# Up projections of a decoder kernel: one product of 512 columns with the high weights, four banks, and stages entered by halves

## The chip, the cores and the metric

The kernel runs on one core of one Trainium2 chip. Its time is the device time of one execution in microseconds (us). Three runs of the kernel before took 1253.54 to 1254.74 us, with a median of 1254.59 us.

## The reference

The reference is a decoder of four layers on one sequence of 256 tokens with 1024 features, all float32. Each layer adds a mixer and then an MLP to x. Layers 0 and 3 have a gated linear recurrence (eight heads), layer 1 block attention, layer 2 a pooling over windows of 2, 4, 8 and 16 tokens.

```python
def rmsnorm(x, gain):
    xf = x.astype(jnp.float32)
    y = xf * lax.rsqrt(jnp.mean(xf * xf, axis=-1, keepdims=True) + RMS_EPS)
    return (y * gain.astype(jnp.float32)).astype(x.dtype)

def sqrelu_mlp(h, w1, w2):          # w1: 1024 x 4096, w2: 4096 x 1024
    a = jax.nn.relu(h @ w1)
    return (a * a) @ w2

for i in range(DEPTH):
    h = rmsnorm(x, norm_mix[i])
    ...                             # y = the mixer of the layer
    x = x + y.astype(x.dtype)
    x = x + sqrelu_mlp(rmsnorm(x, norm_mlp[i]), mlp_w1[i], mlp_w2[i]).astype(x.dtype)
return rmsnorm(x, norm_final)
```

## The kernel before

x is kept transposed, features on the partitions: `xT` has 8 k tiles of 128 features by 256 tokens. A float32 operand goes to TensorE as two numbers of type float32r, a high and a low part. For weights ScalarE writes the high part (`whi`, L929) and VectorE the low part (`wlo = raw - whi`, L1260). For x it is `xh` (L942, with the gain of the norm as its scale) and `xl` (L1271). A product of two such operands is three products: high by high, high by low, low by high. The factor rstd of the norm does not depend on the feature, so it is applied behind the projection; it comes from the sum of squares (`ones_mm`, L453), is made by ScalarE (`rms`), and is turned into a column per token by two transposes (`token_column`, L462, copied into `rcol` by VectorE, L1289).

All weights pass through one ring of two slots, in groups of 2 MB. A group has two units of 1 MB, each loaded by one transfer and split by one ScalarE and one VectorE operation of 128 x 2048. `split(g)` does both units, `split_unit(g, u)` one. Each engine has its own program in the order written here, and waits on semaphores: `lo_done` counts low parts, `bank_ready` finished banks of PSUM, `x_ready` updates of x (four for each addition, of two k tiles each), `xl_done` the low parts of x.

PSUM has eight banks of 512 columns: `hb` (2), `acc` (4) and `misc` (2). `out_banks` are both `hb` and both `misc`.

The MLP of a layer works on 8 pieces of 512 hidden features. The up projection of a piece (`mlp_up`, one group of weights) makes four tiles of 128 features by 256 tokens; `hb[0]` holds tiles 0 and 1, `hb[1]` tiles 2 and 3. For each tile and k tile it issues three products of 256 columns (L559, L560, L561), 96 in all. `hidden` makes the activation for each bank: ScalarE relu (L1217), VectorE multiply by rstd (L1674) and square (L1679), ScalarE high part `hh` (L1223), VectorE low part `hl` (L1681). The down projection of a piece (`mlp_down`, L589 to L591, also 96 products) adds into the four `acc` banks. TensorE's order is up 0, up 1, down 0, then a loop up k+1, down k, and the last down. ScalarE and VectorE have the splits of the coming groups in their order around each `hidden`.

A stage begins with `take_x`: VectorE updates x by two k tiles at a time (L1656 after a mixer, L1717 after an MLP, L1650 after the pooling), ScalarE makes `xh`, VectorE `xl`, and a dictionary says after which step the splits of the next group stand. `group(..., early=...)` issues a mixer's group of weights in two banks; in layer 1 and in the first up projection of each layer the first bank begins with k tiles 0 to 5. `norm_steps` puts `ones_mm` and `token_column` between the quarters of a mixer's first group. In layers 0 and 3 the gates that follow (`gate_a` to `gate_c`) need `rcol`; they run on ScalarE and VectorE in turn, and TensorE's `e_step` (L660) needs their results (`lf_ready`) and those of L1383.

## Time and profile before

| What | Value |
|---|---|
| median of 3 runs | 1254.59 us |
| the profiled execution | 1255.52 us, its span 1253.4 us |
| granted TensorE clock, mean | 0.988 |
| TensorE busy | 1206.9 us (96%), 9363 products |
| VectorE busy | 803.2 us (64%) |
| ScalarE busy | 630.3 us (50%) |
| GpSimd busy | 42.7 us (3%) |
| moved between memory and core | 202.55 MB, mean 162 GB/s |
| `xh` of one k tile (L942), 64 times | mean 499 ns alone, 0.45 us in a pair |
| high part of a unit (L929), 186 times | mean 1903 ns |
| low part of a unit (L1260), 186 times | mean 2317 ns |

The profiled execution is one run with the hardware profiler; its time is a little above its span, which goes from the first to the last instruction. Busy times of TensorE overlap from one product to the next, since a product is still in the array when the next one starts. So the cost of a product in a row of products is the distance of their starts, or a stretch divided by its number of products, and not its mean duration. "Granted clock" is the share of 2.4 GHz that the chip gave to TensorE.

### The profile page before, as it was taken

What the parts mean: (1) busy time and instruction counts of PE and PEld (TensorE: products, weight loads), DVE (VectorE), ACT (ScalarE), POOL (GpSimd) and SP (SyncE); (2) the same over time, 40 slices, a digit from 0 to 9 for tenths busy, and PEclk for the clock granted to TensorE, in tenths of its full rate; (3) what the DMA queues carried; (4) which work ended last, traced back from release to release, by engine and by line L of the source; (5) the groups of instructions that cost most, each with busy time, mean ns of one, the idle gap of its engine ahead of it and who ended that gap; (6) DMA issues with size and microseconds to landing.
All of it is one profiled execution on the core that took longest, in us unless ns stands there. A gap on an engine that the chain in (4) does not pass through costs nothing.

```text
span 1253.4 us, 22191 instructions
## 1 busy us (share of the span) xinstructions
PE 1206.9 (96%) x9363; PEld 1170.1 (93%) x9363; DVE 803.2 (64%) x808; ACT 630.3 (50%) x707; POOL 42.7 (3%) x40
## 2 busy tenths in 40 slices
PE   6999899999999999999997999999989989999997
PEld 5999889999999999999996999999878989999997
DVE  6777767655666656656557675556877767655654
ACT  6955564444453445444435444445885575534441
POOL 2000010000010001000001100000100001000000
PEclk9999999999999999999998899999999999999999
DMA  9442344645356444545445355545433324554520
GB/s 340 153 135 101 101 135 142 225 171 191 144 204 217 142 130 152 202 171 195 171 152 200 124 191 199 192 174 193 160 109 106 121 78 147 191 201 161 200 108 34
DMA packets 84594, 202.55 MB, mean 162 GB/s; under 512 B 3253, under 2 KB 5383, under 8 KB 84272
## 3 DMA queue, kind: packets, MB, share of 16 engines
q1 hardware_dynamic: 84496, 201.58, 46.4%
q8 instruction: 50, 0.82, 0.3%
q14 instruction: 16, 0.13, 0.0%
q0 software_dynamic: 32, 0.02, 0.0%
HBM read 200.52 MB, written 1.06 MB: 161 GB/s over the span
## 4 chain that ended last, share of the span: by engine, by line
PE 84%; DVE 8%; ACT 4%; issue 2%; DMA 1%; SPq 0%; DVEq 0%; ACTq 0%
PE hb L559 10%; PE hb L561 10%; PE hb L560 10%; PE acc L589 9%; PE acc L591 9%; PE acc L590 9%; PE hb L511 4%; PE hb L514 4%; PE hb L513 4%; DVE wlo L1260 3%; PE acc L672 2%; PE hb L527 2%; PE hb L528 2%; PE hb L526 2%; ACT whi L929 1%
## 5 line engine op out<-in xcount | busy, mean ns | idle before, releaser
L1260 DVE TENSOR_TENSOR wlo<-raw,whi 128x2048 fp32r<-128x2048 f32 x186 | 425.1, 2317 | 197.6 <-ACT whi L929 197.5
L929 ACT ACTIVATE whi<-raw 128x2048 fp32r<-128x2048 f32 x186 | 347.0, 1903 | 144.1 <-PE acc L591 121.2
L559 PE MATMUL hb<-xh,whi 128*128 128x256 f32 x1024 | 293.0, 286 | 7.0 <-DVE xT L1656 2.9
L561 PE MATMUL hb<-xh,wlo 128*128 128x256 f32 x1024 | 291.1, 284 | 0.0
L560 PE MATMUL hb<-xl,whi 128*128 128x256 f32 x1024 | 291.1, 284 | 0.0
L589 PE MATMUL acc<-arena_r,whi 128*128 128x256 f32 x1024 | 290.4, 284 | 0.0
L591 PE MATMUL acc<-arena_r,wlo 128*128 128x256 f32 x1024 | 290.0, 283 | 0.0
L590 PE MATMUL acc<-arena_r,whi 128*128 128x256 f32 x1024 | 289.9, 283 | 0.0
L559 PEld LDWEIGHTS hb<-xh,whi 128*128 128x128 f32 x1024 | 197.8, 193 | 8.5 <-DVE xT L1656 3.3
L560 PEld LDWEIGHTS hb<-xl,whi 128*128 128x128 f32 x1024 | 197.8, 193 | 0.1
L561 PEld LDWEIGHTS hb<-xh,wlo 128*128 128x128 f32 x1024 | 197.8, 193 | 0.0
L589 PEld LDWEIGHTS acc<-arena_r,whi 128*128 128x128 f32 x1024 | 196.7, 192 | 0.6 <-DVE wlo L1260 0.6
L591 PEld LDWEIGHTS acc<-arena_r,wlo 128*128 128x128 f32 x1024 | 196.7, 192 | 0.0
L590 PEld LDWEIGHTS acc<-arena_r,whi 128*128 128x128 f32 x1024 | 196.7, 192 | 0.0
L511 PE MATMUL hb<-xh,whi 128*128 128x256 f32 x384 | 111.5, 290 | 0.6 <-DVE wlo L1260 0.5
L514 PE MATMUL hb<-xh,wlo 128*128 128x256 f32 x384 | 108.7, 283 | 0.0
L513 PE MATMUL hb<-xl,whi 128*128 128x256 f32 x384 | 108.6, 283 | 0.0
L1674 DVE TENSOR_TENSOR arena<-arena,rstd 128x512 f32<-128x512 f32 x64 | 44.2, 691 | 89.0 <-ACT arena L1217 71.7
L1217 ACT ACTIVATE arena<-hb 128x512 f32<-128x512 f32 x64 | 38.0, 594 | 121.9 <-PE hb L561 121.9
L1223 ACT ACTIVATE arena_r<-arena 128x512 fp32r<-128x512 f32 x64 | 40.5, 632 | 109.3 <-DVE arena L1679 109.3
L511 PEld LDWEIGHTS hb<-xh,whi 128*128 128x128 f32 x384 | 73.5, 191 | 2.6 <-issue 1.3
L513 PEld LDWEIGHTS hb<-xl,whi 128*128 128x128 f32 x384 | 73.6, 192 | 0.7 <-issue 0.5
(217 smaller groups left out, 1635.5 us busy)
## 6 DMA issues: line engine op xcount, KB each, us to landing
raw<-in_mlp_w_dram SPq DMA_DIRECT2D x128, 1024.0 KB, 5.4
raw<-in_a_w_in_dram SPq DMA_DIRECT2D x32, 1024.0 KB, 5.4
raw<-in_b_w_qkv_dram SPq DMA_DIRECT2D x12, 1024.0 KB, 6.8
raw<-in_a_w_out_dram SPq DMA_DIRECT2D x8, 1024.0 KB, 5.1
raw<-in_b_w_out_dram SPq DMA_DIRECT2D x4, 1024.0 KB, 5.1
arena<-in_x_dram SPq DMA_DIRECT2D x1, 1024.0 KB, 5.3
arena<-in_decay_dram SPq DMA_DIRECT2D x1, 1024.0 KB, 10.8
arena<-bias_rows SPq DMA_DIRECT2D x1, 1024.0 KB, 5.9
```

Of the source, the lines that this page charges most:

```text
L511: pe.matmul(o, h, x_[0][:, kt, :], start=kt == 0 and half == 0, stop=False, skip_group_check=True)
L513: pe.matmul(o, h, x_[1][:, kt, :], start=False, stop=False, skip_group_check=True)
L514: mm = pe.matmul(o, l, x_[0][:, kt, :], start=False, stop=kt == KT - 1, skip_group_check=True)
L559: pe.matmul(o, h, xh[:, kt, :], start=kt == 0 and q == 0, stop=False, skip_group_check=True)
L560: pe.matmul(o, h, xl[:, kt, :], start=False, stop=False, skip_group_check=True)
L561: mm = pe.matmul(o, l, xh[:, kt, :], start=False, stop=kt == KT - 1, skip_group_check=True)
L589: pe.matmul(o, h, hh[:, par, kt, :], start=st, stop=False, skip_group_check=True)
L590: pe.matmul(o, h, hl[:, par, kt, :], start=False, stop=False, skip_group_check=True)
L591: mm = pe.matmul(o, l, hh[:, par, kt, :], start=False, stop=last and kt == 3, skip_group_check=True)
L929: act.activation(whi[:, g % 2, u, 0:n], raw[:, g % 2, u, 0:n], ACT.Copy).then_inc(hi_done, 1)
L1260: dve.tensor_tensor(wlo[:, g % 2, u, 0:n], raw[:, g % 2, u, 0:n], whi[:, g % 2, u, 0:n].bitcast(F32), ALU.subtract).then_inc(lo_done, 1)
L1674: dve.tensor_tensor(act_s[:, i, :].rearrange("p (a b) -> p a b", a=2), act_r[:, i, :].rearrange("p (a b) -> p a b", a=2), rstd[:, :].rearr ...
```

## The change

`xh` and `xl` become two halves of one tensor `xhl`, side by side within each k tile, so that one product takes both as 512 columns. In the up projection each of the four tiles of 128 features has a bank of its own: columns 0 to 255 get high by high and low by high, columns 256 to 511 high by low. `hidden` adds the two halves. The banks are both `hb` and both `misc`; the sum of squares ahead of an MLP goes to `acc[3]` instead of `misc[0]`, and layer 1's and layer 2's mixers write their results to the four banks of `out_banks`.

A stage's first group is entered by halves: first k tiles 0 to 3 of every tile or bank, then 4 to 7. With this the splits stand at other places in `take_x`, and the sum of squares and the transposes come one quarter later.

```diff
-        xh = sb("xh", [P, KT, SEQ], F32R)
-        xl = sb("xl", [P, KT, SEQ], F32R)
+        xhl = sb("xhl", [P, KT, 2, SEQ], F32R)
+        xh, xl = xhl[:, :, 0, :], xhl[:, :, 1, :]
...
+        up_pairs = [hb_pair, misc_pair]
+        def ms_bank(n):
+            return acc[3] if n % 2 else misc[0]
...
                 def step():
                     at[0] += 1
-                    if at[0] == 2:
+                    if at[0] == 3:
                         ones_mm(n)
-                    if at[0] == 3:
+                    if at[0] == 4:
                         token_column(n)
...
+                if early:
+                    for q in range(2):
+                        for i in range(2):
+                            if q == 0:
+                                last_read(k + i)
+                            if kind == "T":
+                                for f in range(2):
+                                    mm = t_block(g, banks[i], f, 2 * i + f, need, 4 * q, 4 * q + 4, x_)
+                            else:
+                                mm = w_half(g, banks[i], i, 4 * q, 4 * q + 4, need)
+                            if q:
+                                mm.then_inc(bank_ready, 1)
+                            between()
+                    return
...
-                        pe.matmul(o, h, xh[:, kt, :], start=kt == 0 and q == 0, stop=False, skip_group_check=True)
-                        pe.matmul(o, h, xl[:, kt, :], start=False, stop=False, skip_group_check=True)
-                        mm = pe.matmul(o, l, xh[:, kt, :], start=False, stop=kt == KT - 1, skip_group_check=True)
+                        pe.matmul(o[:, :], h, xhl[:, kt, :, :], start=kt == 0, stop=False, skip_group_check=True)
+                        mm = pe.matmul(o[:, 0:SEQ], l, xh[:, kt, :], start=False, stop=kt == KT - 1,
+                                       skip_group_check=True)
...
+                if r_at is None:
+                    for half in range(2):
+                        for f in range(4):
+                            if half == 0:
+                                pe.wait_ge(x_ready, 4 * (2 * layer + 1) + 1 + f)
+                            mm = tile(f, 4 * half, 4 * half + 4)
+                            if half and f % 2:
+                                mm.then_inc(bank_ready, 1)
+                    return
                 for i in range(2):
-                    if r_at is not None:
-                        pe.wait_ge(relu_done, r_at + (i - 1))
...
+                    pe.wait_ge(summed, r_at + (i - 1))
                     for q in range(2):
-                        mm = tiles(i, q, k0, KT)
+                        mm = tile(2 * i + q, 0, KT)
...
-                    group("W", g0, 0, acc_read, need, norm_steps(n), acc[0:2])
+                    group("W", g0, 0, acc_read, need, norm_steps(n), acc[0:2], early=True)
...
ScalarE
-                take_x(n + 1, {} if layer % 3 == 2 else {1: lambda: split(g)})
+                take_x(n + 1, {} if layer % 3 == 2 else {1: lambda: split_unit(g, 0), 5: lambda: split_unit(g, 1)})
...
-                        act.activation(act_r[:, i, :], hb[i][:, :], ACT.Relu).then_inc(relu_done, 1)
+                        act.activation(act_u[:, i, :].rearrange("p (a b) -> p a b", a=2), up_pairs[i][:, :, SEQ:2 * SEQ],
+                                       ACT.Copy).then_inc(low_sb, 1)
                         if first and i == 0:
                             rms(n + 1)
...
+                        act.activation(act_s[:, i, :], act_u[:, i, :], ACT.Square)
...
                         act.activation(hh[:, par, 2 * i:2 * i + 2, :],
-                                       act_s[:, i, :].rearrange("p (a b) -> p a b", a=2), ACT.Copy)\
+                                       act_u[:, i, :].rearrange("p (a b) -> p a b", a=2), ACT.Square)\
                             .then_inc(hh_done, 1)
...
VectorE
-                split(g0 + 1)
-                if layer % 3 != 1:
+                split_unit(g0 + 1, 0)
+                if layer % 3 == 2:
+                    column(n)
+                else:
+                    split_unit(g0 + 1, 1)
+                if layer % 3 == 0:
                     column(n)
...
+                    split_unit(g0 + 1, 1)
                     dve.wait_ge(inv_in, 16)
...
-                take_x(n + 1, mixed, {} if layer % 3 == 2 else {1: lambda: split(g)})
+                take_x(n + 1, mixed, {} if layer % 3 == 2 else {1: lambda: split_unit(g, 0), 2: lambda: split_unit(g, 1)})
...
-                        dve.tensor_tensor(act_s[:, i, :].rearrange("p (a b) -> p a b", a=2),
-                                          act_r[:, i, :].rearrange("p (a b) -> p a b", a=2),
-                                          rstd[:, :].rearrange("p (a b) -> p a b", a=1).to_broadcast([P, 2, SEQ]),
-                                          ALU.mult).then_inc(scaled_done, 1)
-                        dve.wait_ge(scaled_done, r_at + (i + 1))
-                        dve.tensor_tensor(act_s[:, i, :], act_s[:, i, :], act_s[:, i, :], ALU.mult).then_inc(s_done, 1)
+                        z = act_u[:, i, :].rearrange("p (a b) -> p a b", a=2)
+                        dve.wait_ge(low_sb, r_at + (i + 1))
+                        dve.tensor_tensor(z, up_pairs[i][:, :, 0:SEQ], z, ALU.add)\
+                            .then_inc(summed, 1)
+                        if first and i == 0:
+                            dve.wait_ge(rstd_ready, n + 2)
+                        dve.wait_ge(summed, r_at + (i + 1))
+                        dve.scalar_tensor_tensor(out=z, in0=z, scalar=0.0,
+                                                 in1=rstd[:, :].rearrange("p (a b) -> p a b", a=1)
+                                                 .to_broadcast([P, 2, SEQ]),
+                                                 op0=ALU.max, op1=ALU.mult).then_inc(scaled_done, 1)
```

TensorE, where layer 0's up projection begins; `misc` is a bank of the output projection that ends there. Before:

```order
L514 MATMUL misc<-arena_r,wlo 128x256
L559 MATMUL hb<-xh,whi 128x256 [waits lo_done,xl_done,x_ready]
L560 MATMUL hb<-xl,whi 128x256
L561 MATMUL hb<-xh,wlo 128x256
L559 MATMUL hb<-xh,whi 128x256 [waits xl_done]
L560 MATMUL hb<-xl,whi 128x256
```

and now:

```order
L517 MATMUL misc<-arena_r,wlo 128x256
L573 MATMUL hb<-xhl,whi 128x512 [waits lo_done,xl_done,x_ready]
L574 MATMUL hb<-xhl,wlo 128x256
L573 MATMUL hb<-xhl,whi 128x512 [waits xl_done]
L574 MATMUL hb<-xhl,wlo 128x256
L573 MATMUL hb<-xhl,whi 128x512 [waits xl_done]
L574 MATMUL hb<-xhl,wlo 128x256
```

Three products of 256 columns per step have become one of 512 and one of 256.

VectorE, from the first x update after layer 0's mixer to the first low parts of the MLP's second group. Before:

```order
L1656 TENSOR_TENSOR xT<-hb,xT 128x512 x2
L1271 SCALAR_TENSOR_TENSOR xl<-xT,gains,xh 128x256 x2
L1260 TENSOR_TENSOR wlo<-raw,whi 128x2048 x2
L1656 TENSOR_TENSOR xT<-misc,xT 128x512
L1271 SCALAR_TENSOR_TENSOR xl<-xT,gains,xh 128x256 x2
L1656 TENSOR_TENSOR xT<-misc,xT 128x512
L1271 SCALAR_TENSOR_TENSOR xl<-xT,gains,xh 128x256 x4
```

and now:

```order
L1686 TENSOR_TENSOR xT<-hb,xT 128x512 x2
L1296 SCALAR_TENSOR_TENSOR xhl<-xT,gains,xhl 128x256 x2
L1285 TENSOR_TENSOR wlo<-raw,whi 128x2048
L1686 TENSOR_TENSOR xT<-misc,xT 128x512
L1296 SCALAR_TENSOR_TENSOR xhl<-xT,gains,xhl 128x256 x2
L1285 TENSOR_TENSOR wlo<-raw,whi 128x2048
L1686 TENSOR_TENSOR xT<-misc,xT 128x512
L1296 SCALAR_TENSOR_TENSOR xhl<-xT,gains,xhl 128x256 x4
```

The second unit's low part has moved from ahead of the third update to ahead of the fourth.

VectorE in layer 2, from the last update of x by layer 1's MLP to the first pooling result (L1641, now L1671). Before:

```order
L1717 TENSOR_TENSOR xT<-acc,xT 128x512
L1271 SCALAR_TENSOR_TENSOR xl<-xT,gains,xh 128x256 x4
L1260 TENSOR_TENSOR wlo<-raw,whi 128x2048 x2
L1289 COPY rcol<-misc 128x2
L1629 SCALAR_TENSOR_TENSOR arena_r<-acc,rcol,arena_r 128x512 x4
L1641 TENSOR_TENSOR arena<-hb,arena 128x512
```

and now:

```order
L1747 TENSOR_TENSOR xT<-acc,xT 128x512
L1296 SCALAR_TENSOR_TENSOR xhl<-xT,gains,xhl 128x256 x4
L1285 TENSOR_TENSOR wlo<-raw,whi 128x2048
L1314 COPY rcol<-misc 128x2
L1658 SCALAR_TENSOR_TENSOR arena_r<-acc,rcol,arena_r 128x512 x4
L1285 TENSOR_TENSOR wlo<-raw,whi 128x2048
L1671 TENSOR_TENSOR arena<-hb,arena 128x512
```

The second low part has moved from ahead of the column's copy to behind the four operations that use it.

## Rows read from the trace of the kernel before

**Rows 1.** The page's chain that ended last, shares of the span by engine.

```profile
PE 84%; DVE 8%; ACT 4%; issue 2%; DMA 1%; SPq 0%; DVEq 0%; ACTq 0%
```

**Rows 2.** Groups: line, engine, operation, out<-in, count | busy us, mean ns | idle before.

```profile
L559 PE MATMUL hb<-xh,whi 128*128 128x256 f32 x1024 | 293.0, 286 | 7.0 <-DVE xT L1656 2.9 <-DVE xT L1650 2.3 <-DVE xl L1271 1.8
...
L1674 DVE TENSOR_TENSOR arena<-arena,rstd 128x512 f32<-128x512 f32 x64 | 44.2, 691 | 89.0 <-ACT arena L1217 71.7 <-ACT rstd L957 17.3
...
L1223 ACT ACTIVATE arena_r<-arena 128x512 fp32r<-128x512 f32 x64 | 40.5, 632 | 109.3 <-DVE arena L1679 109.3
L1217 ACT ACTIVATE arena<-hb 128x512 f32<-128x512 f32 x64 | 38.0, 594 | 121.9 <-PE hb L561 121.9
```

**Rows 3.** TensorE's waits: who <- whom: us in total, times, longest.

```profile
PE acc L660 <- DVE arena L1383: 4.8, 1, 4.8
...
PE hb L511 <- DVE wlo L1260: 0.5, 1, 0.5
```

**Rows 4.** Stretches, layer 0's third up projection: busy us of each engine, clock, DMA.

```profile
218.99:230.51 11.52, 11.52 (x99) 11.52 (x97) 6.66 (x6) 4.95 (x4) 0.00 (x0) 1.00 0.96 317
```

**Rows 5.** TensorE in time, layer 0's first stage: start us, duration us, engine, line.

```profile
30.12 0.39 PE L527 MATMUL acc<-wlo,xh 128*128 128x512 f32 x1
...
40.54 0.39 PE L528 MATMUL acc<-whi,xl 128*128 128x512 f32 x1
```

**Rows 6.** ScalarE and VectorE in time, after the third up projection.

```profile
233.56 3.70 ACT L929 ACTIVATE whi<-raw 128x2048 fp32r<-128x2048 f32 x2
...
235.50 4.49 DVE L1260 TENSOR_TENSOR wlo<-raw,whi 128x2048 fp32r<-128x2048 f32 x2 [1.11 <-ACT whi L929]
```

**Rows 7.** TensorE in time, layer 0's first up projection to the second.

```profile
182.35 0.39 PE L559 MATMUL hb<-xh,whi 128*128 128x256 f32 x1 [1.44 <-DVE xT L1656]
184.68 0.39 PE L559 MATMUL hb<-xh,whi 128*128 128x256 f32 x1 [0.51 <-DVE xl L1271]
...
194.88 1.03 PE L453 MATMUL misc<-hn,ones 128*128 128x256 f32 x4
195.56 0.47 PE L559 MATMUL hb<-xh,whi 128*128 128x256 f32 x1
```

**Rows 8.** VectorE in time, the same place.

```profile
177.20 4.49 DVE L1260 TENSOR_TENSOR wlo<-raw,whi 128x2048 fp32r<-128x2048 f32 x2 [0.33 <-ACT whi L929]
...
183.43 0.68 DVE L1656 TENSOR_TENSOR xT<-misc,xT 128x512 f32<-128x512 f32 x1
...
187.84 5.27 DVE L1260 TENSOR_TENSOR wlo<-raw,whi 128x2048 fp32r<-128x2048 f32 x2 [2.02 <-ACT whi L929]
```

**Rows 9.** Layer 2 in time, TensorE and VectorE; last a stretch as in Rows 4.

```profile
677.35 0.44 PE L462 MATMUL misc<-ident,rstd 128*128 128x128 f32 x2 [1.01 <-ACT rstd L957]
681.87 2.50 PE L878 MATMUL hb<-whi,arena_r 128*128 128x256 f32 x10 [4.07 <-DVE arena_r L1629]
693.82 0.58 PE L559 MATMUL hb<-xh,whi 128*128 128x256 f32 x1 [0.78 <-DVE xl L1271]
706.12 1.03 PE L453 MATMUL misc<-hn,ones 128*128 128x256 f32 x4
...
679.43 0.15 DVE L1289 COPY rcol<-misc 128x2 f32<-128x2 f32 x1
684.05 0.69 DVE L1641 TENSOR_TENSOR arena<-hb,arena 128x512 f32<-128x512 f32 x1 [0.92 <-PE hb L878]
...
690.80:706.10 15.30, 14.45 (x96) 14.16 (x97) 9.30 (x12) 6.96 (x8) 2.58 (x2) 0.78 0.51 172
```

**Rows 10.** Layer 3's mixer in time, TensorE and VectorE.

```profile
879.98 0.40 PE L526 MATMUL acc<-whi,xh 128*128 128x512 f32 x1
890.19 0.38 PE L462 MATMUL misc<-ident,rstd 128*128 128x128 f32 x2
937.08 0.58 PE L660 MATMUL acc<-decay,arena_r 128*128 128x256 f32 x1 [4.80 <-DVE arena L1383]
...
890.69 0.15 DVE L1289 COPY rcol<-misc 128x2 f32<-128x2 f32 x1
```

More of the change, by code:

```diff
@@ L202, in build_decoder @@
         scaled = carve(2048, 2, 512)
-        act_r = carve(0, 2, 512)
+        act_u = carve(0, 2, 512)
         act_s = carve(1024, 2, 512)
@@ L487, in need_x @@
                     pe.wait_ge(xl_done, 8 * n + f + 1)
-            def x_banks(n):
-                def wait(k):
-                    if k >= 2:
-                        pe.wait_ge(x_ready, 4 * n + k - 1)
-                return wait
             def mixer_banks(layer, first=0):
@@ L532, in group @@
                       early=False):
+                if early:
[12 more added lines that the diff above has]
+                    return
                 for i in range(2):
                     last_read(k + i)
-                    if early and i == 0:
-                        for q in range(2):
-                            t_block(g, banks[i], q, 2 * i + q, need, 0, 6, x_)
                     for q in range(2):
                         if kind == "T":
-                            mm = t_block(g, banks[i], q, 2 * i + q, need, 6 if early and i == 0 else 0, KT, x_)
+                            mm = t_block(g, banks[i], q, 2 * i + q, need, 0, KT, x_)
                         else:
@@ L549, in mlp_up, with tile @@
             def mlp_up(layer, g, lo_at, r_at=None):
-                def tiles(i, q, k0, k1):
-                    o = hb[i][:, q * SEQ:(q + 1) * SEQ]
+                def tile(f, k0, k1):
+                    o = out_banks[f]
                     for kt in range(k0, k1):
                         need_x(2 * layer + 1, kt)
-                        if i == 0 and q == 0 and kt % 4 == 0:
+                        if f == 0 and kt % 4 == 0:
                             pe.wait_ge(lo_done, lo_at + (kt // 4 + 1))
-                        h, l = (w_k(t, g, kt, (2 * i + q) * P, (2 * i + q + 1) * P) for t in (whi, wlo))
-                        pe.matmul(o, h, xh[:, kt, :], start=kt == 0 and q == 0, stop=False, skip_group_check=True)
-                        pe.matmul(o, h, xl[:, kt, :], start=False, stop=False, skip_group_check=True)
-                        mm = pe.matmul(o, l, xh[:, kt, :], start=False, stop=kt == KT - 1, skip_group_check=True)
-                    return mm
@@ L564, in mlp_up @@
-                for i in range(2):
-                    if r_at is not None:
-                        pe.wait_ge(relu_done, r_at + (i - 1))
-                    else:
-                        pe.wait_ge(x_ready, 4 * (2 * layer + 1) + 3 + i)
-                    k0 = 0
-                    if r_at is None and i == 0:
-                        k0 = 6
-                        for q in range(2):
-                            tiles(i, q, 0, k0)
+                        h, l = (w_k(t, g, kt, f * P, (f + 1) * P) for t in (whi, wlo))
@@ L844, in _ @@
                     for c in range(2):
-                        group("T", go + c, 2 * c, x_banks(n + 1), need_o_once, x_=(oh, ol))
+                        group("T", go + c, 2 * c, lambda k: None, need_o_once, banks=out_banks[2 * c:2 * c + 2],
+                              x_=(oh, ol))
                 elif layer % 3 == 2:
```

42 lines of the change are left out of this document (23 added, 19 removed).

## The prediction, made before the changed kernel ran

> **What bounds the kernel now.** The chain of waits was read first: 84% of it is TensorE [rows 1]. The list of groups then says what TensorE does. The up projection issues 1024 products of each of three kinds [rows 2]. The list of TensorE's waits has 16 rows that add up to 41.4 us, of which two stand here; nearly all the rest of the 1253.4 us is products back to back [rows 3]. For such a stretch the table of stretches is the view that counts, because the "mean ns" of a product overlaps its neighbours: one up projection in the loop has 96 products and lasts 11.52 us, so a product of 256 columns costs 120.0 ns of issue at the full granted clock of 1.00 [rows 4]. In that stretch VectorE is busy 6.66 us and ScalarE 4.95 us. TensorE sets the pace there, and a shorter up projection moves the end unless its helpers or its weights come late.
>
> **The merged product.** Its form, 512 columns with whi or wlo on one side and x on the other, is in the trace: in layer 0's first stage 47 such products follow each other from 30.12 to 40.54 us, 46 steps, so 226.5 ns each [rows 5]. At 2.4 GHz, the level which that clock means, 256 and 512 columns take 106.7 and 213.3 ns, so both forms carry some 13.3 ns that don't grow with the columns. Two products of 256 (240.0 ns) become one of 512 (226.5 ns): 13.5 ns less, 1024 times, 13.8 us in all, or 0.43 us for each of 32 groups. The ends are far apart: 0 if the new product costs as much as the two that it replaces, 27 us if it went at the bare 213.3 ns. The rows have the same form, and with starts to 0.01 us over 46 steps they leave about 0.3 ns open, so I take 0.43 us a group. The Trainium skill speaks against this: "TensorE: Matmul & The Clock Gate", section Back-to-back issue gap, gives N/2.4 + 2.5 ns for warm products. By that a merge saves 2.5 ns, 2.6 us in all. The trace disagrees with that rule by 10.8 ns on both forms, so I stay with the rows.
>
> **The helpers inside the loop.** Per half group, before: ScalarE relu (0.594 us), VectorE multiply and square, ScalarE copy to the high part (0.632 us), VectorE subtract. After: ScalarE copies the low halves out (taken as the relu's 0.594), VectorE adds, then one operation with max and rstd (0.69 each, as now), ScalarE squares twice (0.63 each), VectorE subtracts. [rows 2] have these durations. That is one ScalarE operation more: 64 x 0.63 = 40 us of ScalarE work, all beside TensorE. What it delays: after the second half of a group ScalarE starts the next weights' high part at 233.56, and VectorE ends their low part at 235.50 + 4.49 = 239.99; TensorE wants its second half at 242.03 (the down group's end, 230.51 + 11.52) + 1.44 [rows 6]. The chain grows by one square less overlap, 0.55 us, which leaves 2.9 us. Reading two banks by one operand is in no row; from one bank the same VectorE work takes 0.69 us and ScalarE's 0.594 us, and I take these. Weights come in time too: a loop round of 22.6 us needs 4.2 MB, 186 GB/s, and 317 GB/s were moved in the stretch of [rows 4].
>
> **The entry into the up projection, layers 0 and 3.** Now TensorE waits 1.44 + 0.51 us there [rows 7]. It goes over to k tiles 0 to 3 of all four output tiles first, so it can start when the output projection ends, about 180.9. But the second half of the weights' split (half of 4.49 us [rows 8]) moves behind the third x update on VectorE, and the fourth update stands behind it: third update 179.4 to 180.1, xh of tiles 4 and 5 (0.45 us each), the high part on ScalarE (half of 3.70 us [rows 6]) to 182.9, the low part to 185.2, fourth update to 185.9. Before, that update ended at 183.43 + 0.68 = 184.1. Tiles f = 0, 1, 2 last 3 x 1.39 us, to 185.1; f = 3 waits for x_ready until 185.9, then 1.39 and the second halves' 5.55 us: end 192.9 instead of 194.88. That is 2.0 us won. Then it is given back. The second up group now waits on VectorE's sum of the first, and VectorE has the next group's low parts ahead of that sum. Those end now at 187.84 + 5.27 = 193.11; with xh of tiles 6 and 7 1.8 us later, they end at 194.9, and the sum at 195.6. TensorE had started that group at 195.56. Net zero for each of the two layers, the 0.43 us of this first group included; the bounds are 0.7 us either way per layer. In layer 1 nothing waits at this place and its fourth bank is late anyway (the low parts end before the group does), so its group simply gives 0.43.
>
> **Layer 2, the pooling stage.** The column of rstd is copied ahead of the second low split, and can follow the transpose (677.35 + 0.44) instead of 679.43 [rows 9]: 1.6 us earlier, and TensorE's pooling products start at 680.3 instead of 681.87. But the split now stands between those results and the first x update: 681.5 to 683.8, so that update starts at 683.8 against 684.05. Only 0.25 us is left of the 1.6. From there VectorE's chain is the old one. TensorE wants x tiles 2 and 3, 691.1, for all but 2 of the 32 steps (a step is 0.347 us); before, it stood until 693.82 with 4 steps' worth done. 30 steps are 10.4 us; the granted clock was 0.78 over this stretch, so part of it goes at 1.2 GHz. After 693.82 that cost 706.12 - 693.82 - 84 x 0.120 = 2.2 us; from 691.1 on it can cost 2.2 to 3.6. End at 703.7 to 705.1 instead of 706.12; I take 1.7 us, of which 0.43 is already counted: 1.3 more.
>
> **The entry into layer 3's mixer.** Here the order by halves costs something. The sum of squares and the transpose move one quarter back, behind 36 and 48 wide products instead of 24 and 36. The transpose comes at 879.98 + 48 x 0.2265 + 0.8 (the two products for the sum) = 891.7 instead of 890.19, and rstd's column at 892.3 instead of 890.69 [rows 10]. The chain of waits from 890.69 to 937.08 holds ScalarE and VectorE alone, gate by gate, and TensorE stands 4.80 us at its end. So 1.6 us is added to the time, and what TensorE gains ahead of it only lengthens its wait. In layers 0 and 1 the same shift (2.4 and 2.6 us) meets no such wait: no row of TensorE's waits lies between the first stages and the last outputs there. In layer 0 some 0.2 us of small waits for x tiles goes.
>
> **The sum.** 30 groups x 0.43 = 12.9; layers 0 and 3 at their first group 0; layer 2 another 1.3; layer 0's start 0.2; layer 3's column -1.6. Together 12.8 us. The profiled execution took 1255.52 us (span 1253.4), so 1242.7; it stood 0.93 above the median of the runs, 1254.59, which gives 1241.8.
>
> **Rivals.** (a) The gaps at the stage entries are worse than I read: the wait of the second up group comes in all four layers (in layers 1 and 2 the sum stands behind the same low parts, but these end 1.3 us before TensorE arrives), or layer 3's gates slip by more. At 1.5 us each in four places the gain shrinks to about 7: 1247.6. For it speaks that VectorE's queue decides at each of these places; against it, the margins above. (b) The product over x's two halves keeps the fixed cost of both, 240.0 ns, and the merge brings nothing. Then the other terms are left, layer 2's 1.3 with its group's 0.43 gone and layers 0 and 3 0.43 longer each, about 1.2 us longer than now: 1255.8, within 0.2% of the median. The products of [rows 5] speak against it. The rule of the Trainium skill named above would end near this case, some 2.6 us ahead of it. (c) The slower side: the helpers' chain becomes the loop's bound. It decides once the chain grows by more than 0.55 + 2.9 us; with both copies and both sums over two banks 1.2 us longer than over one, it is 4.8 us longer, 1.9 us over per group, and 28 groups lose 53 us: 1295. No row reads two banks at once, so it can't be excluded; that a row with strides inside one bank costs the same 0.69 us as a plain one speaks against it. (d) The change doesn't do what it says, and x's halves don't stream as one run of 512: the halves of a k tile lie next to each other, so I give it nothing beyond (b).
>
> **Chances and range.** Forecast 0.75, (a) 0.15, (b) 0.06, (c) 0.04. The forecast's own terms: 0.3 either way for the merge, 1.4 at layers 0 and 3, 1.4 at layer 2, 1 at layer 3: 1238 to 1246, if they all fall one way. The range, 1237.5 to 1246.8, takes in nearly half of (a) as well. About 0.2% (2.5 us) is what a measurement of this kernel tells from no change. Faster by more than that: 0.92; within: 0.05; slower: 0.03.
>
> **What would show it.** Right: an up group in the loop of 11.09 us and a down group still of 11.52; in layers 0 and 3 a wait of 0.8 us for the fourth x update and one of about 2 us ahead of the second up group; in layer 3 a wait near 6.4 us or more where 4.80 stood, with the 0.5 us of [rows 3] grown to some 3 ahead of it; in layer 2 a first pooling product at 1.6 us after an earlier column. Wrong: an up group of 11.4 us or more (b), waits of TensorE inside the loop (c), or entry waits that add up to over 4 us more than now (a).

## The result, and the profile after

The changed kernel takes 1247.29 us (median of 5 runs, 1246.50 to 1248.39). The kernel before, run on the same chip, took 1253.66 us. The ratio is 0.9949, with a 95% interval of 0.9937 to 0.9961: faster by 6.4 us. The forecast was 1241.8 us, so half of the forecast gain is missing, and the time lies just above the range.

The profiled execution took 1247.29 us too, with a span of 1245.1 us and a mean granted clock of 0.992. First the stretches: the third up group of layer 0, as in [rows 4], and from there to the eighth up group, five up and five down groups in turn, without a wait. The columns are as in [rows 4].

After:

```profile
217.30:228.60 11.30, 11.30 (x66) 9.81 (x65) 7.15 (x6) 5.47 (x5) 0.00 (x0) 1.00 0.95 328
...
217.30:331.43 114.13, 114.13 (x803) 106.64 (x802) 65.92 (x51) 54.16 (x50) 0.00 (x0) 1.00 0.54 191
```

Before, the second of them:

```profile
218.99:334.19 115.20, 115.20 (x963) 115.20 (x961) 65.71 (x51) 48.91 (x40) 0.00 (x0) 1.00 0.54 190
```

The down groups in them still take 11.52 us. Five up groups are 1.07 us shorter, 0.21 us each, where the forecast has 0.43. A group of 32 steps lasts 11.31 us (11.30 in the row, whose ends are rounded), and a step, one wide product of 512 columns and one narrow one of 256, takes 353.4 ns. The forecast has 226.5 + 120.0 = 346.5. TensorE in time (start, duration, engine, line) shows the steps:

```profile
217.30 0.40 PE L573 MATMUL hb<-xhl,whi 128*128 128x512 f32 x1
217.54 0.28 PE L574 MATMUL hb<-xhl,wlo 128*128 128x256 f32 x1
217.66 0.40 PE L573 MATMUL hb<-xhl,whi 128*128 128x512 f32 x1
217.90 0.28 PE L574 MATMUL hb<-xhl,wlo 128*128 128x256 f32 x1
218.01 0.39 PE L573 MATMUL hb<-xhl,whi 128*128 128x512 f32 x1
218.24 0.28 PE L574 MATMUL hb<-xhl,wlo 128*128 128x256 f32 x1
```

From start to start, a wide product takes 0.23 to 0.24 us here; over all such places of the trace the mean is 236.3 ns for it and 117.6 ns for the narrow one. The wide one is 10 ns dearer than in [rows 5], the narrow one 2 ns cheaper than in [rows 4].

The groups of the helpers (busy us, mean ns, idle before) answer [rows 2]:

```profile
L1702 DVE TENSOR_TENSOR arena<-misc,arena 128x512 f32<-128x512 f32 x32 | 22.1, 689 | 52.8 <-ACT arena L1238 52.8
L1707 DVE SCALAR_TENSOR_TENSOR arena<-arena,rstd 128x512 f32<-128x512 f32 x64 | 44.3, 692 | 8.5 <-ACT rstd L978 6.2
...
L1245 ACT ACTIVATE arena<-arena 128x512 f32<-128x512 f32 x64 | 40.5, 632 | 105.6 <-DVE arena L1707 105.6
L1238 ACT ACTIVATE arena<-misc 128x512 f32<-128x512 f32 x32 | 19.0, 594 | 55.0 <-PE misc L574 55.0
```

Reading two banks by one operand costs what reading one does: 594 ns on ScalarE, 689 on VectorE. TensorE waits nowhere inside the loop. Its waits that have to do with the change (total, times, longest) are all at entries:

```profile
PE acc L675 <- DVE arena L1412: 4.8, 1, 4.8
PE hb L573 <- DVE arena L1702: 2.8, 2, 1.4
PE hb L573 <- DVE xhl L1296: 2.5, 1, 2.5
PE hb L514 <- DVE wlo L1285: 2.0, 1, 2.0
PE hb L573 <- DVE xT L1680: 1.9, 1, 1.9
PE misc L573 <- DVE xT L1686: 1.6, 2, 1.0
PE acc L604 <- DVE wlo L1285: 1.4, 2, 0.7
```

The first row is layer 3's mixer, as in [rows 3]. L1702, twice 1.4 us, is the sum ahead of the second up group, in layers 0 and 3. L1686 is the fourth x update there. L1296 and L1680 are layer 2's x. L604, twice 0.7 us, is new: in layers 1 and 2 the first down group waits for the low part of its second unit.

### The profile page after: what moved, and what is told of

Read it like the earlier page. It is cut to its first block, busy times and chain, and to the rows that moved or that the text cites. A ratio compares the mean times of both kernels' runs of the same rounds, so it can differ in the third digit from the quotient of the medians.

```text
span 1245.1 us, 20130 instructions
## 1 busy us (share of the span) xinstructions
PE 1197.4 (96%) x8339; PEld 1113.9 (89%) x8339; DVE 801.2 (64%) x808; ACT 663.9 (53%) x771; POOL 41.5 (3%) x40
## 4 chain that ended last, share of the span: by engine, by line
PE 81%; DVE 8%; ACT 5%; issue 3%; DMA 1%; SPq 0%; POOL 0%; DVEq 0%; ACTq 0%
PE acc L604 9%; PE acc L605 9%; PE acc L606 9%; PE hb L573 9%; PE misc L573 9%; PE hb L574 4%; PE misc L574 4%; PE hb L514 3%; PE hb L517 3%; PE hb L516 3%; DVE wlo L1285 3%; PE acc L687 2%; ACT whi L950 2%; PE hb L531 2%; PE hb L530 2%
## 5 line engine op out<-in xcount | busy, mean ns | idle before, releaser
L604 PE MATMUL acc<-arena_r,whi 128*128 128x256 f32 x1024 | 290.0, 283 | 1.4 <-DVE wlo L1285 1.4
L604 PEld LDWEIGHTS acc<-arena_r,whi 128*128 128x128 f32 x1024 | 196.3, 192 | 3.2 <-DVE wlo L1285 1.8
L573 PE MATMUL hb<-xhl,whi 128*128 128x512 f32 x512 | 184.8, 403 | 7.2 <-DVE arena L1702 2.8
L573 PE MATMUL misc<-xhl,whi 128*128 128x512 f32 x512 | 183.5, 400 | 1.6 <-DVE xT L1686 1.6
L574 PE MATMUL hb<-xhl,wlo 128*128 128x256 f32 x512 | 144.5, 282 | 0.0
L574 PE MATMUL misc<-xhl,wlo 128*128 128x256 f32 x512 | 144.1, 281 | 0.0
L573 PEld LDWEIGHTS hb<-xhl,whi 128*128 128x128 f32 x512 | 97.1, 190 | 31.1 <-DVE arena L1702 3.6
L573 PEld LDWEIGHTS misc<-xhl,whi 128*128 128x128 f32 x512 | 96.7, 189 | 26.2 <-DVE xT L1686 2.3
L514 PE MATMUL hb<-xhl,whi 128*128 128x256 f32 x352 | 102.9, 292 | 2.0 <-DVE wlo L1285 2.0
L516 PE MATMUL hb<-xhl,whi 128*128 128x256 f32 x352 | 100.2, 285 | 0.0
L517 PE MATMUL hb<-xhl,wlo 128*128 128x256 f32 x352 | 100.2, 285 | 0.0
L574 PEld LDWEIGHTS hb<-xhl,wlo 128*128 128x128 f32 x512 | 97.7, 191 | 0.1
L574 PEld LDWEIGHTS misc<-xhl,wlo 128*128 128x128 f32 x512 | 97.1, 190 | 0.0
L1712 DVE TENSOR_TENSOR arena_r<-arena,arena_r 128x512 fp32r<-128x512 f32 x64 | 44.3, 692 | 78.0 <-ACT arena_r L1248 78.0
L514 PEld LDWEIGHTS hb<-xhl,whi 128*128 128x128 f32 x352 | 68.0, 193 | 2.9 <-DVE wlo L1285 2.2
```

The source lines that it names most:

```text
L514: pe.matmul(o, h, x_[0][:, kt, :], start=kt == 0 and half == 0, stop=False, skip_group_check=True)
L516: pe.matmul(o, h, x_[1][:, kt, :], start=False, stop=False, skip_group_check=True)
L517: mm = pe.matmul(o, l, x_[0][:, kt, :], start=False, stop=kt == KT - 1, skip_group_check=True)
L573: pe.matmul(o[:, :], h, xhl[:, kt, :, :], start=kt == 0, stop=False, skip_group_check=True)
L574: mm = pe.matmul(o[:, 0:SEQ], l, xh[:, kt, :], start=False, stop=kt == KT - 1, skip_group_check=True)
L604: pe.matmul(o, h, hh[:, par, kt, :], start=st, stop=False, skip_group_check=True)
```

## The experiments

All kernels below are the changed kernel with one edit, unless the text says otherwise. TensorE's mean granted clock differs from execution to execution, also of one kernel (0.986 to 0.992 over the five of the changed kernel), and medians carry that with them; the table at the end of this section compares at one clock. Two theories stood at the start. "Alternation": the wide product costs what [rows 5] say only among its like. "Form": with weights stationary, x streaming and a whole bank written, it costs 236 ns anywhere.

### Wide products first, then the narrow ones

```diff
+   for kt in range(k0, k1): wide(kt)        # whi x xhl, 512 columns
+   for kt in range(k0, k1): narrow(kt)      # wlo x xh, 256 columns
-   for kt in range(k0, k1): wide(kt); narrow(kt)
```

> The changed kernel, but within a tile of the up projection the 8 (or, at a layer's entry, 4) wide products of 512 columns go first and then the 8 narrow ones; same products, same banks. In the changed kernel a wide and a narrow product alternate and a pair takes 353.4 ns, an up group in the loop 11.31 us. Theory 'alternation' (a wide product costs about 229.5 ns among its like, as the mean over layer 0's first stage says, a narrow one 120.0, and only the change of width costs the rest): up group 4 x 8 x (229.5 + 120.0) = 11.18 us, the whole 30 x 0.13 = 3.8 us shorter, about 1243.5 us. Theory 'form' (512 columns of x against a stationary tile of weights, into a whole bank, costs 236 ns wherever it stands): up group still 11.31 us and 1247.3 us. My recorded 226.5 ns would give 11.09 us and about 1240.7 us.

Measured: 1245.25 us, ratio 0.9943 (0.9929 to 0.9956), groups in the loop of 11.17 us. Two tiles in time:

```profile
219.97 2.00 PE L574 MATMUL hb<-xhl,whi 128*128 128x512 f32 x8
221.81 1.11 PE L577 MATMUL hb<-xhl,wlo 128*128 128x256 f32 x8
222.77 2.00 PE L574 MATMUL misc<-xhl,whi 128*128 128x512 f32 x8
```

Eight wides take 1.84 us, 230 ns each, the eight narrows 0.96, 120. Over 112 tiles the steps of the wides are 233, 236, 228, 233, 231, 227, 227 and 227 ns, and the first narrow takes 113.5 ns. The order alone changes the price, so "form" is out. Only 2 us came of the 3.8: wides wait for the low weights here though they don't use them, and the third up groups of layers 1 and 2 took 11.55 and 11.58 us. These two account for 0.8 us; the rest was not traced.

### Nothing but wide products

The product with the low weights takes both halves of x as well, which is one product (low by low) more than the kernel needs.

```diff
-   mm = pe.matmul(o[:, 0:SEQ], l, xh[:, kt, :], ...)
+   mm = pe.matmul(o[:, :], l, xhl[:, kt, :, :], ...)
```

> The changed kernel, but the product with the low weights takes both halves of x too (512 columns, which adds low by low), so the up projection is 64 products of 512 columns a group and nothing else. It measures the wide product of this form among its like. 'Alternation': 64 x 229.5 ns = 14.69 us a group, 32 x 3.38 = 108 us more, about 1355 us. 'Form': 64 x 236 = 15.10 us, about 1369 us. By my recorded 226.5 ns: 14.50 us, about 1349 us. TensorE at 213.3 ns, if nothing but the columns counted: 13.65 us, 1322 us.

Measured: 1340.99 us; the group and a few of its products:

```profile
221.01:235.55 14.54, 14.54 (x67) 12.02 (x66) 6.57 (x5) 5.47 (x5) 0.00 (x0) 1.00 0.66 247
```

```profile
222.63 0.39 PE L574 MATMUL hb<-xhl,wlo 128*128 128x512 f32 x1
222.85 0.39 PE L573 MATMUL hb<-xhl,whi 128*128 128x512 f32 x1
223.08 0.39 PE L574 MATMUL hb<-xhl,wlo 128*128 128x512 f32 x1
223.31 0.39 PE L573 MATMUL hb<-xhl,whi 128*128 128x512 f32 x1
```

64 products in 14.53 us, 227.0 ns each. So the 226.5 ns of the forecast hold for this form, too, with high and low weights in turn and x streaming; what they don't hold for is a wide product between narrow ones. The total is 8 to 14 us under what I expected from the group times, partly because slower up groups leave no waits at L604, L1702 and L1686 (5.8 us in the changed kernel).

### The merge alone undone

```diff
-   pe.matmul(o[:, :], h, xhl[:, kt, :, :], ...)
+   pe.matmul(o[:, 0:SEQ], h, xh[:, kt, :], ...)
+   pe.matmul(o[:, SEQ:2 * SEQ], h, xl[:, kt, :], ...)
```

> The changed kernel with everything kept (banks, entries by halves, helpers) except the merge: the product of 512 columns is two products of 256, high by high into the first half of the bank, high by low into the second. Theory 'the merge was mis-sized' (it is worth 0.21 us a group, and the entries gave what was forecast): up group 11.52 us, 30 to 32 x 0.21 = 6.3 to 6.7 us more than 1247.3, so 1253.6 to 1254.0 us, level with the kernel before. Rival 'the entries' (the merge gave its full 13 us and the entries lost 6): about 1260 us. Rival 'two products into different halves of a bank cost less': up group under 11.5 us and a time under 1253.

Measured: 1254.27 us (11 runs), ratio 1.0007 (0.9998 to 1.0016), group 11.52 us. The merge is worth 7.0 us in this kernel, 6.8 by its steps (1024 x (360.0 - 353.4) ns). All the rest of the change together is worth nothing, or 0.9 us to the worse. The two rivals on record are out: the time is not near 1260 us, and two products into different halves of a bank take 120.0 ns each as before.

### The narrow product into the other half of the bank

```diff
-   mm = pe.matmul(o[:, 0:SEQ], l, xh[:, kt, :], ...)
+   mm = pe.matmul(o[:, SEQ:2 * SEQ], l, xh[:, kt, :], ...)
```

> The changed kernel, but the narrow product (low by high) adds into columns 256 to 511 of the bank instead of 0 to 255; the sum over the halves is the same. Theory 'bank' (a narrow product behind a wide one is slow, or makes the next wide slow, because it adds into the columns that the wide one has just written): pair under 353.4 ns, up group towards 11.10 us, up to 6 us shorter. Theory 'width' (the change of width or of weights' pace costs it): 353.4 ns, 11.31 us and 1247.3 us.

Measured: 1247.80 us in one run, group 11.31 us, wide 236.2 ns. Which columns of the bank the narrow product adds to doesn't matter.

### Two and two, sixteen and sixteen, thirty-two and thirty-two

First two wide products and two narrow ones in turn:

> The changed kernel with two wide products, then two narrow ones, and so on. 'Settling' (the first two wides after a narrow 233 and 236 ns, the first two narrows 113.5 and 119 ns): 701.5 ns for two pairs, up group 11.22 us. 'Only strict alternation costs': 2 x 347.0, 11.10 us. 'Form or interleaving at all': 11.31 us as in the changed kernel. Time by settling about 1247.3 - 30 x 0.09 = 1244.6 us.

Measured: 1244.17 us (one run), group 11.15 us, a pair of products 348.8 ns: less than settling gives, more than "only strict alternation". Both sizes were wrong; the second wide took 233 ns, not 236.

Then 16 and 16 for each pair of banks, at the layers' entries as well, and the wides wait for the high weights alone:

```diff
+   for f in (2 * i, 2 * i + 1): 8 wides      # wait for hi_done
+   for f in (2 * i, 2 * i + 1): 8 narrows    # wait for lo_done
```

> The changed kernel with the products of a bank pair grouped (16 wides that wait for the high weights only, then 16 narrows) and nothing else changed: the part of 'combined' (1241.0 us) that is the grouping. Group in the loop 11.13 us as there, 30 x 0.18 = 5.4 us under the changed kernel: 1241.9 us. If so, the other edits of 'combined' (gates 1.5, waits 4.0) gave only 1 us. Rival: those edits did give about 3 us or more and the grouping costs at the entries; then this run is at 1244 us or above.

Measured: 1243.37 us, ratio 0.9925 (0.9911 to 0.9938), group 11.13 us. That lies between the two expectations. With 20 groups in the loops, 3.4 us of it are the loops' by the trace (each stretch from the third to the eighth up group 113.27 us, after 114.13).

And 32 and 32, over all four banks:

```diff
+   pe.wait_ge(summed, r_at)                  # both bank pairs
+   32 wides over four banks, then 32 narrows
```

> The changed kernel, but an up group in the loop issues all 32 wide products first (four banks), then all 32 narrow ones; wides wait for the high weights only, narrows for the low ones. The runs so far: wides among their like 227.0 ns, narrows 120.0, a pair in alternation 353.4, and with 8 and 8 a pair 349.1, where the first five wides after a narrow take 233, 236, 228, 233, 231 ns and then 227. Theory 'settling' (after each change of width some 16.5 ns are lost in all, over several products): group 32 x 347.0 + 16.5 ns = 11.12 us, 30 x 0.19 = 5.7 us under the changed kernel, about 1241.6 us. Rival 'every wide in this form costs about 230 and only an alternating one more': 11.2 us, 1244 us. Rival 'helpers': the first two banks are finished 3.6 us later, ScalarE and VectorE get late, TensorE waits inside the loop, and the time is above wide_first's 1245.3 us.

Measured: 1267.80 us, ratio 1.0120 (1.0105 to 1.0135): 20 us slower than the changed kernel, though its loop group is the shortest, 11.11 us, as "settling" says. The list of waits has the reason; it is a late helper, but at the layers' entries and not in the loop as the rival had it:

```profile
PE hb L572 <- DVE arena L1702: 18.1, 4, 4.8
```

The second up group now waits for the sums over both bank pairs of the first, four times up to 4.8 us. And that isn't all of it. TensorE in time, and the stretch behind the wait:

```profile
197.67 6.21 PE L572 MATMUL hb<-xhl,whi 128*128 128x512 f32 x16 [4.78 <-DVE arena L1702]
```

```profile
197.67:203.67 6.00, 6.00 (x16) 4.76 (x17) 3.67 (x4) 4.75 (x4) 0.00 (x0) 0.59 0.23 84
```

After the wait the granted clock was 0.59 for 6 us, so most of it went at 1.2 GHz, and the 16 wides took 6.05 us to the start of the next product (203.72), where they take 3.65 at 2.4 GHz. This wait of 4.8 us cost 7.2.

### Layer 3's sum of squares back at its old place

```diff
-   if at[0] == 3:                      # ones_mm
+   if at[0] == (2 if n == 6 else 3):
-   if at[0] == 4:                      # token_column
+   if at[0] == (3 if n == 6 else 4):
```

> The changed kernel, but in layer 3's mixer the sum of squares and the transpose stand behind the second and third quarter of the first group again, as in the kernel before. If layer 3's gates hang on the column of rstd alone, as forecast, it comes about 1.5 us earlier and the time falls by 1.5 us to about 1245.8 us. Rival: with the first group entered by halves, the sum of squares isn't ready behind the second quarter; TensorE waits there, the column comes as late as now, and the time stays at 1247.3 us or rises by up to 1 us.

Measured: 1246.94 us, ratio 0.9952 (0.9938 to 0.9965), not told apart from the changed kernel by time. The trace tells more. In the changed kernel the mixer's first product, the column and the end of the long wait stand at (TensorE, VectorE, TensorE; answers to [rows 10]):

```profile
872.15 0.40 PE L529 MATMUL acc<-whi,xhl 128*128 128x512 f32 x1
...
884.39 0.16 DVE L1314 COPY rcol<-misc 128x2 f32<-128x2 f32 x1 [1.44 <-PE misc L472]
...
930.77 0.58 PE L675 MATMUL acc<-decay,arena_r 128*128 128x256 f32 x1 [4.80 <-DVE arena L1412]
```

and with this edit at:

```profile
872.19 0.40 PE L529 MATMUL acc<-whi,xhl 128*128 128x512 f32 x1
...
882.89 0.14 DVE L1314 COPY rcol<-misc 128x2 f32<-128x2 f32 x1
...
929.28 0.55 PE L675 MATMUL acc<-decay,arena_r 128*128 128x256 f32 x1 [4.80 <-DVE arena L1412]
```

Column 12.24 against 10.70 us after the first product, end of the wait 58.62 against 57.09: the gates take the 1.5 us through unchanged. The profiled spans differ by 1.4 us (1245.1, 1243.7). That the medians show 0.35 lies within their scatter of 1.6 to 1.9 us; at one clock the difference is 1.6 us (table below). The rival named a wait of TensorE for the sum of squares: it is there, 0.9 us, and the column comes earlier all the same.

### The old order of the first up group

```diff
-   for half in range(2): for f in range(4): tile(f, 4 * half, 4 * half + 4)
+   tiles 0, 1: k tiles 0 to 5; tiles 0, 1: k tiles 6, 7; tiles 2, 3: all 8
-   {1: split_unit(g, 0), 2: split_unit(g, 1)}
+   {1: split(g)}
```

> The changed kernel with the up projection's first group of every layer entered as before (tiles 0 and 1 with k tiles 0 to 5, then 6 and 7, then tiles 2 and 3 whole) and both units of its weights split behind the second x update. My prediction said of the entry by halves: net zero in layers 0 and 3 within 0.7 us each, 1.3 us gained in layer 2. By that this kernel takes 1.3 us more, 1248.6 us, with no wait for the fourth x update and a first group that starts up to 2 us later in layers 0 and 3. Rival: the halves win at the entry and it is not given back (the wait for the sum is there with either order), then 3 us or more: 1250.5 us or above. Rival: they cost, since the sum behind the low parts is later by them: 1246 us or less.

Measured: 1253.73 us (11 runs, 1250.60 to 1254.81), ratio 1.0000 (0.9990 to 1.0009). By the medians the halves are worth 6.4 us in this kernel, not 1.3; but a part of that is clock. TensorE's waits:

```profile
PE hb L573 <- DVE xhl L1299: 7.9, 6, 2.5
...
PE acc L607 <- DVE wlo L1288: 2.2, 4, 0.7
```

The profiled spans differ by 5.6 us (1250.7, 1245.1). From the first product of a layer's first up group to its third up group the old order costs 0.79, 0.05, 1.10 and 2.20 us in layers 0 to 3. Of that, 0.73 and 0.75 us are longer first down groups in layers 0 and 3 (waits of L607). In layer 3 the first up group took 1.4 us longer at a clock of 0.79, which the other kernel doesn't have there:

```profile
1052.00:1060.00 8.00, 7.49 (x34) 6.20 (x33) 5.95 (x7) 6.07 (x6) 2.57 (x2) 0.79 0.38 143
```

Another 1.4 us of layer 0 are such a stretch near 155 us, ahead of this edit. So the entries by themselves make 4.1 us of the 5.6, or 2.7 without layer 3's stretch, and at one clock the executions differ by 4.3 us (table below). Whether the old order brings some of the lower clock itself is not shown; its 11 executions have a median clock of 0.983. This is also not a return to the kernel before: with a bank for each tile the first product starts earlier than in [rows 7] and then stands for x.

### The fourth x update ahead of the split

```diff
-   {1: split_unit(g, 0), 2: split_unit(g, 1)}     # VectorE; ScalarE 5 -> 7
+   {1: split_unit(g, 0)};  split_unit(g, 1) behind the last x tile
```

> The changed kernel, but in layers 0, 1 and 3 the second unit of the up projection's first group is split behind the fourth x update (ScalarE behind the high parts of all x tiles, VectorE behind all their low parts) instead of ahead of it. In the changed kernel VectorE stands 1.55 us idle ahead of that split while the fourth update waits behind it, TensorE waits 0.67 and 0.95 us for that update in layers 0 and 3, and 1.4 us each for the sum over the first bank pair ahead of the second up group. Theory 'queue order': the two waits for the update go, everything behind it on VectorE comes some 2 us earlier and the two waits of 1.4 go as well; TensorE may now stand up to 1.1 us for the low weights at the second half. Together 2 to 4 us less: 1243.3 to 1245.3 us. Rival: the entry is bound by the weights' split anyway, a wait of the same size stands at L573 for wlo, and the time stays at 1247.3 us.

Measured: 1246.84 us, ratio 0.9944 (0.9930 to 0.9958). The waits for the update went, and the low weights and the sum took their place:

```profile
PE hb L573 <- DVE wlo L1285: 1.8, 3, 0.9
...
PE hb L573 <- DVE arena L1704: 1.3, 3, 0.5
```

The rival had the place of the new waits right: a reordering passes part of the wait on while the next product needs the low weights at once. Not all of it, though, and the median hides that. By the trace, from the first up product to the third up group, the edit saves 1.1 us in layer 0 and 1.1 in layer 3 and costs 0.5 in layer 1, 1.7 us in all (layer 2 is left as it was); ahead of the first up group this profile has lower clocks than the changed kernel's. At one clock it is 2.0 us ahead.

### What the runs point to, in one kernel

```diff
+   16 wides (hi_done), 16 narrows (lo_done) for each bank pair
+   layer 3: sum of squares and transpose one quarter earlier
+   down: the 8 products with whi of a tile, then the 4 with wlo (lo_done)
+   VectorE: split_unit(g + 1, 0), sum of the first pair, split_unit(g + 1, 1)
```

> The changed kernel with: 16 wides then 16 narrows per bank pair, wides waiting for the high weights only; layer 3's sum of squares and transpose one quarter earlier; in the down projection the two products with high weights of all four k tiles ahead of the four low ones; at a layer's first up group VectorE's sum over the first bank pair between the two low parts of the next group instead of behind both. By the runs: up group 2 x (16 x 347.0 + 16.5) ns = 11.14 us, 30 x 0.17 = 5.1 us; layer 3's gates 1.5; the waits of 0.7 us at L604 in layers 1 and 2 mostly gone, 1.2; the waits of 1.4 us in layers 0 and 3 gone, 2.8. Sum 10.6, about 1236.7 us. If the waits are only passed on to the next place (VectorE is behind by its whole amount of work): 1247.3 - 5.1 = about 1242 us.

Measured: 1240.99 us, ratio 0.9896 (0.9881 to 0.9911), nearer to "passed on" (1242) than to the sum (1236.7). The waits of 1.4 us went, but the down groups of layers 0 and 3 got 0.76 us longer, and two waits of 0.7 us for the fourth update stayed. With the split behind that update added:

> 'combined' plus the split of the first up group's second unit behind the fourth x update (the edit of fourth_first). Alone that edit moved the time by less than 0.5 us, because TensorE then stood 1.8 us for the low weights at the second halves and 1.3 us for the sum. With the 8 wides of the second half ahead of the narrows TensorE wants the low weights 1.8 us later, when they are there. Theory 'cover': the waits of 1.3 us for the fourth update and of 1.3 us for the low part of the first down group go: 1238.4 to 1239.7 us. Rival 'VectorE is behind by its work': they come back at the second up group's sum and the time stays at 1241.0 us.

Measured: 1235.95 us (4 runs, 1235.65 to 1237.83), ratio 0.9867 (0.9852 to 0.9882): 17.4 us faster than before, and under the 1238.4 that was the best expected. No wait for the fourth update is left, and of those at the first down groups this:

```profile
PE acc L611 <- DVE wlo L1290: 0.7, 4, 0.2
```

By the medians the same edit brought 0.5 us alone and 5.0 us here. Most of that contrast is clock: by the traces, at the entries, it is 1.7 alone and 2.5 here (1.26 in layer 0 and 1.25 in layer 3, with layer 1's loss gone). Of the 5.2 us between the two profiled spans another 1.5 are the stretch from 152 to 160 us, at a clock of 1.00 here and 0.57 in "combined".

### The same comparisons at one clock

The mean granted clock is known for 101 executions, of all these kernels and of the kernel before. A line with one slope for all and a constant for each kernel gives 0.30 us less for every 0.001 more clock; the last column is an estimate from it, with 95% intervals of 0.7 to 1.0 us.

| Compared | medians, us | at one clock, us |
|---|---|---|
| changed kernel less kernel before | -6.4 | -5.5 |
| merge undone less changed kernel | +7.0 | +6.4 |
| old entry less changed kernel | +6.4 | +4.3 |
| layer 3's sum of squares early | -0.35 | -1.6 |
| fourth update first, alone | -0.5 | -2.0 |
| the same within "combined" | -5.0 | -3.9 |
| sixteen and sixteen | -3.9 | -5.1 |

The changed kernel's five executions had the highest mean clock of the kernels run five times, 0.990, so comparisons with its median are unkind to the edits. The slope is no constant of the chip, and an edit that adds waits may lower the clock itself; the column only shows which differences a median alone does not carry.

## Why the prediction was wrong, point by point

- **The step that failed is the merge's price.** "Two products of 256 (240.0 ns) become one of 512 (226.5 ns): 13.5 ns less." The mechanism was right and the size was off: 6.6 ns (353.4 against 360.0), 0.21 us a group instead of 0.43. [rows 5] is a row of wide products only, and a wide product among wide ones costs 227.0 ns in the new form as well. The new stream alternates 512 and 256 columns, and nothing in the trace of before does. I carried the price over without saying that the neighbours change, and gave the term 0.3 us of play, where ends of 0 and 27 us had been named. With 0.21 in place of 0.43, my sum of 12.8 becomes 6.2 us; 6.4 were measured, and 5.5 at one clock, so an agreement within 0.2 us is in part luck.
- **The rule of the Trainium skill** ("TensorE: Matmul & The Clock Gate", Back-to-back issue gap) puts N/2.4 + 2.5 ns between warm products, and calls that the gap of isolated ones, which the prediction left out. My estimate from it was 2.5 ns for each product saved, 2.6 us in all. The merge measured 6.6 ns a pair, 6.8 us. The measurement lies between the rule and my rows, nearer to the rule than I allowed. In streams of one width the rule stays off by some 11 ns a product (120.0 and 227.0 ns).
- **Helpers in the loop: right.** The high part of the next weights starts 3.4 us after the group's end (232.03 - 228.60; before 3.05 by [rows 4, 6]), 0.4 us more where 0.55 was forecast, and nothing waits. Two banks at once cost nothing extra, so rival (c) is out by the 594 and 689 ns.
- **Layers 0 and 3: right.** There is a wait of 0.67 and 0.95 us for the fourth update (0.8 forecast), a first group that ends early, and 1.4 us ahead of the second (about 2). In layer 3 the changed kernel leads by 6.31 us at the long wait's end and by 6.45 at the second up group: net 0.1.
- **Layer 2: right.** The transpose leads by 5.02 us (677.35, 672.33), the end of the first up group by 6.87 (706.12, 699.25): 1.85 us won, 1.7 forecast. The first pooling product came at 675.25 after a column at 672.80:

```profile
672.80 0.16 DVE L1314 COPY rcol<-misc 128x2 f32<-128x2 f32 x1 [0.52 <-PE misc L472]
...
675.25 3.43 PE L899 MATMUL hb<-whi,arena_r 128*128 128x256 f32 x16 [2.48 <-DVE arena_r L1658]
```

- **Layer 3: right in size, wrong in the wait it named.** 1.5 us were lost (1.6 forecast). But the long wait stayed at 4.80 us instead of 6.4, and the low weights' wait grew from 0.5 to 2.0 and came one place earlier, not to 3. The low part stands among the gates' operations on VectorE and comes with them 1.5 us later (it ends at 898.66; with the earlier column it begins at 894.88 instead of 896.38). So TensorE loses the 1.5 us there already and reaches the long wait that much later; the forecast let the same delay lengthen both waits.
- **Not foreseen:** twice 0.7 us at the first down group of layers 1 and 2. A faster TensorE reaches VectorE's low part sooner; the forecast stopped at the second up group.
- **Rival (a)** had 1247.6 us, close to the time, for a reason that is hardly there. The waits at the entries into the MLPs add up to 10.2 us (the rows above without layer 3's mixer, 4.8 and 2.0) against 7.0 before, 3.2 more and less than the 4 that were its sign. And the terms other than the merge gave what was forecast: "unmerged" is 0.9 us slower than before, where rival (b), the same case, says 1.2 (its terms add up to 1.0). The time alone would have spoken for (a).
- The profiled pair differs by 8.2 us, the medians by 6.4. The stretch from 152 to 160 us, told below, can be 0.8 us of these 1.8. The rest stays open: the profiled execution of the kernel before was slow for its clock (1255.52 us at 0.988).

## What to carry to other kernels

The price of an instruction in a stream depends on its neighbours: take it from rows where the same sequence stands, and where the change makes a sequence that no row has, keep both ends in the range. If two widths must be mixed, group them (8 and 8, or even 2 and 2, brought back two thirds or more of the loss), and let each wait only for what it reads. At a stage entry part of a removed wait comes back as the wait queued behind it, until that one has cover too: by the traces 1.7 us alone, 2.5 with cover. And where an effect is as small as the scatter of the granted clock, compare stretches that the clock leaves alone, or executions at the same clock: the medians said 0.5 and 5.0.

## What the runs showed of the hardware that was not expected

- Start to start at a granted clock of 1.00: 256 columns among their like 120.0 ns, 512 among theirs 227.0; strictly alternating 236 and 117.5, a pair 353.4; two and two 348.8; eight and eight 349.1. After a run of narrow products wides need five steps until they reach 227 ns. Weights (high or low) and the half of the bank written make no difference. What in TensorE causes it stays open.
- The same instructions at two clocks: TensorE waits 3.3 us in layer 0's mixer, until 153.91 us in the changed kernel and 154.35 in the kernel before. Over the stretch from 152 to 160 us the granted clock was 0.79 in the kernel before and 1.00 in the changed one. The kernel with the narrow product in the other half of the bank doesn't differ from the changed one until the first up projection at 180 us, and it had 0.57.

The changed kernel, then that one:

```profile
152.00:160.00 8.00, 6.09 (x40) 5.13 (x41) 2.82 (x4) 6.55 (x10) 0.00 (x0) 1.00 0.44 134
```

```profile
152.00:160.00 8.00, 5.81 (x25) 5.62 (x26) 2.68 (x5) 5.82 (x8) 0.00 (x0) 0.57 0.42 134
```

Of the 14 profiled kernels nine fell there and five did not. From the end of that wait to the first up projection it is 25.8 us in the five, 26.1 to 26.6 in those at 0.79 (without the 1.44 us that the kernel before waits there for x), and 27.2 to 27.6 in those at 0.57 to 0.61. A pair of profiles can differ by up to 1.8 us here with no edit behind it. What decides whether the clock falls is not shown.
